# Two attention loops of a hybrid block: latent heads scored in pairs, and the first NSA head ahead of the compressed sums

## What is computed

```python
# NSA branch, 8 heads of 128; with 256 tokens every 64-block is selected
s = einsum('bqgrd,bngd->bgrqn', qb, kc) * scale            # 15 compressed keys
o_cmp = einsum('bgrqn,bngd->bqgrd', masked_softmax(s, ...), vc)
...                                                        # causal softmax over ks, vs: o_slc
...                                                        # causal softmax over kw, vw: o_win
o = gb[..., 0:1] * o_cmp + gb[..., 1:2] * o_slc + gb[..., 2:3] * o_win

# latent branch, 8 heads; 128 plain and 64 rotated dimensions of query and key
q_b = rms_norm(q_b, mla_q_norm)
k_b = rms_norm(k_b, mla_k_norm)
s = jnp.einsum('bqhd,bkhd->bhqk', qb, k) * scale           # over 192 dimensions
p = masked_softmax(s, kpos[None, :] <= t[:, None])
o = jnp.einsum('bhqk,bkhd->bqhd', p.astype(v.dtype), v)

x = x + gate_a * ((g_a * o_a + g_b * o_b) @ w_o)
```

## Times and profile before

| | us |
|---|---|
| median of 3 runs | 1046.87 |
| lowest, highest | 1045.39, 1047.06 |
| the profiled execution | 1046.69 |
| its span | 1044.9 |

### The profile page before, as it was taken

One profiled execution on the slowest core, in us unless ns is written; L12 is line 12 of the kernel. 1 busy time (PEld: TensorE's weight loads), 2 busy tenths in 40 slices (PEclk: granted clock), 3 DMA queues, 4 the chain that ended last, 5 costly groups with the idle time before them and its releaser, 6 DMA issues.

```text
span 1044.9 us, 23159 instructions
## 1 busy us (share of the span) xinstructions
PE 1017.8 (97%) x8513; PEld 960.6 (92%) x8513; DVE 556.5 (53%) x1167; ACT 619.9 (59%) x1118; POOL 688.9 (66%) x306
## 2 busy tenths in 40 slices
PE   7999999999999999999999999999989999999998
PEld 4899999988899989999999899998567699999998
DVE  2577724579875445555631642288576744444400
ACT  4565764477784466666654556754575556666642
POOL 2498898822249875988798388880041076988795
PEclk9999999999999999999999999999999999999999
DMA  9988788756357882777778379966211044656563
GB/s 379 380 300 279 272 305 296 258 183 210 133 176 233 284 295 88 273 241 236 238 238 273 109 272 351 365 233 209 84 60 41 1 153 128 209 195 196 163 214 113
DMA packets 62616, 226.43 MB, mean 217 GB/s; under 512 B 6960, under 2 KB 8272, under 8 KB 61264
## 3 DMA queue, kind: packets, MB, share of 16 engines
q1 hardware_dynamic: 61344, 221.23, 61.3%
q10 hardware_dynamic: 1200, 4.23, 1.3%
HBM read 224.35 MB, written 1.08 MB: 216 GB/s over the span
## 4 chain that ended last, share of the span: by engine, by line
PE 79%; issue 6%; POOL 5%; DVE 4%; ACT 4%; DMA 1%; ACTq 0%; DVEq 0%; POOLq 0%
PE psL L560 73%; POOL WL L512 5%; PE psO L560 3%; PE psS L560 2%; ACT WH L1178 1%; DMA ring<-wts 1%; PE psL L1115 1%; DVE SQ L2379 1%; ACT R L1296 0%; DVE X L2089 0%; DVE sm L2297 0%; PE psS L1061 0%; DVE psL L2088 0%; ACT psL L1719 0%; DVE sm L2296 0%
## 5 line engine op out<-in xcount | busy, mean ns | idle before, releaser
L512 POOL TENSOR_TENSOR WL<-ring,WH 128x1024 fp32r<-128x1024 f32 (+1 forms) x282 | 669.5, 2393 | 226.6 <-ACT WH L1178 176.9
L560 PE MATMUL psL<-HR,WH 128*128 128x256 f32 (+1 forms) x3096 | 514.1, 278 | 1.9 <-DVE HR L1834 1.1
L560 PEld LDWEIGHTS psL<-HR,WH 128*128 128x128 f32 (+1 forms) x3096 | 452.9, 187 | 7.7 <-issue 4.8
L560 PE MATMUL psL<-HR,WL 128*128 128x256 f32 x1536 | 396.5, 277 | 0.0
L1178 ACT ACTIVATE WH<-ring 128x1024 fp32r<-128x1024 f32 (+1 forms) x210 | 216.5, 1042 | 106.3 <-PE psL L560 71.3
L560 PEld LDWEIGHTS psL<-HR,WL 128*128 128x128 f32 x1536 | 275.3, 188 | 0.0
L560 PE MATMUL psL<-RR,WH 128*128 128x256 f32 x1356 | 205.3, 277 | 2.8 <-DVE RR L2019 1.2
L560 PEld LDWEIGHTS psL<-RR,WH 128*128 128x128 f32 x1356 | 185.3, 187 | 4.5 <-issue 2.8
L560 PE MATMUL psL<-RR,WL 128*128 128x256 f32 x672 | 144.9, 277 | 0.3 <-POOL WL L512 0.3
L2117 DVE SCALAR_TENSOR_TENSOR CT<-psL,par,CT 128x254 f32<-128x254 f32 (+1 forms) x176 | 80.8, 480 | 107.9 <-ACT CT L1490 102.8
L1481 ACT ACTIVATE WH<-ring 128x1024 fp32r<-128x1024 f32 (+1 forms) x88 | 92.9, 1058 | 71.6 <-PE psL L560 62.9
(11 more groups left out here) (278 smaller groups left out, 1091.7 us busy)
## 6 DMA issues: line engine op xcount, KB each, us to landing
ring<-wts SPq DMA_DIRECT2D x285, 512.0 KB, 4.2
adaring<-ada_w SPq DMA_DIRECT2D x80, 512.0 KB, 4.5
R<-ada_w SPq DMA_DIRECT2D x8, 1024.0 KB, 16.3
ring<-wts SPq DMA_DIRECT2D x16, 384.0 KB, 3.9
R<-cum_dram ACTq DMA_DIRECT2D x8, 512.0 KB, 4.2
R<-wts SPq DMA_DIRECT2D x8, 512.0 KB, 6.6
ring<-wts SPq DMA_DIRECT2D x8, 288.0 KB, 3.2
adaring<-wts SPq DMA_DIRECT2D x4, 512.0 KB, 6.8
```

Of the source, the lines that this page charges most:

```text
L512: nc.gpsimd.tensor_tensor(WL[:, k, 0:n], ring[:, k, 0:n], WH[:, k, 0:n].bitcast(F32), SUB).then_inc(lo_done, 1)
L560: return nc.tensor.matmul(out, lhsT, rhs, start=start, stop=stop)
```

## The change

Four edits.

- Layout: `QB` and `KB` hold all plain dimensions of the eight heads first, then all rotated ones (before, 192 columns a head). So two heads' rotated parts lie side by side, 128 columns, and are transposed at once: head 2k lands on partitions 0 to 63 and head 2k+1 on 64 to 127, queries and keys of both in one unit, copied by VectorE into `MR`. The turns have 12 units in place of 16. ScalarE copies the query units in two pieces, VectorE applies the query gain in two.
- Latent scores in pairs (`mla_pair`): plain products of both heads, then the rotated products of both, one on the lower and one on the upper 64 rows, then both masks. A pair takes two banks. Pairs 0 and 1 are issued in steps 0 and 1, four heads in four banks; pairs 2 and 3 behind the transposes of steps 3 and 5 and ahead of the values of these steps.
- The maximum of NSA head 0 stands on VectorE ahead of the compressed sums, its exponential on ScalarE behind that of the compressed scores; the compressed probabilities are finished behind the scaling of head 0 and the maximum of head 1 (`compressed_probabilities`, called from `nsa_outs(1)`). The transposes of the compressed probabilities move from step 2 to step 3 of TensorE's loop and from a scratch bank to `psO`, and ScalarE's copy of them from behind the exponential of head 1 to behind that of head 3.
- `second_layer_values` moves from behind key-value unit 1 to behind unit 3.

```diff
-PLAN.bare("mla_turns", 16)
+PLAN.bare("mla_turns", 12)
...
-                if n == 1:
-                    second_layer_values()
                 if n == 2:
                     turn_compressed_keys()
+                if n == 3:
+                    second_layer_values()
...
                 for i in range(min(first, 2), count + 3):
                     if first <= i < count:
-                        masked_scores(p0 + i, i, score)
-                    if i == 2 and lead_in:
+                        scores(i)
+                    if i == 3 and lead_in:
                         turn_cmp()
...
+                    if behind:
+                        behind(i)
                     if i >= 3:
...
-            for i in range(16):
-                pair, kind = divmod(i, 4)
+            for i in range(12):
+                pair, kind = divmod(i, 3)
...
+                    if kind == 1:
+                        src = (QB, KB)[hh][:, t, NH * HD + pair * P:NH * HD + (pair + 1) * P]
...
+            def mla_scores(i):
+                if i < 2:
+                    mla_pair(i)
+            def mla_behind(i):
+                if i in (3, 5):
+                    mla_pair((i + 1) // 2)
+            def mla_pair(pair):
+                i = 2 * pair
+                pe.wait_ge(turned, 8 + 2 * pair + 2)
+                pe.wait_ge(rope_turned, pair + 1)
+                outs = []
+                for e in range(2):
+                    u = head_unit(16 + i + e)
+                    bank_wait(u)
+                    outs.append(psL[:, u % 4, :])
+                for q0, lo, hi in ((0, 0, P), (P, P, 384)):
+                    for e in range(2):
+                        mm(outs[e][:, lo:hi], MQN[:, i + e, q0:q0 + P], MKN[:, i + e, 0:hi - lo], True, False)
+                    for e in range(2):
+                        r = ROPE * e
+                        mm(outs[e][:, lo:hi], MR[r:r + ROPE, pair, q0:q0 + P], MR[r:r + ROPE, pair, T:T + hi - lo], False, False)
+                    for e in range(2):
+                        last = mm(outs[e][:, hi - P:hi], identb[:, :], maskb[:, :], False, True)
+                        if q0 == P:
+                            last.then_inc(lin_done, 1)
...
-                if n == 6:
+                if n == 7:
                     act.wait_ge(cs_ready, 1)
                     cs3 = CS.rearrange("p (m n) -> p m n", n=32)[:, :, 0:NCMP]
                     A(cs3, cs3, ACT.Exp).then_inc(ce_ready, 1)
+                    head_exp(0, [1.0, 1.0])
...
-                    if n == 1:
+                    if n == 3:
                         turned_cmp()
...
             dve.sem_inc(cs_ready, 1)
+            head_max(0)
+            key_gain(6)
             dve.wait_ge(ce_ready, 1)
...
+                if i == 1:
+                    head_max(1)
+                    compressed_probabilities()
```

More of the change, by code:

```diff
@@ L1046, in _, with attend @@
                 masked_scores(n, n, nsa_score)
-            def attend(name, pname, obase, count, score, value, lead_in, p0, first=0, follow=None):
+            def attend(name, pname, obase, count, scores, value, lead_in, p0, first=0, follow=None, behind=None):
                 for i in range(min(first, 2), count + 3):
                     if first <= i < count:
-                        masked_scores(p0 + i, i, score)
-                    if i == 2 and lead_in:
+                        scores(i)
+                    if i == 3 and lead_in:
                         turn_cmp()
@@ L1083, in turn_cmp @@
                     for t in range(2):
-                        last = nc.tensor.transpose(out[:, g * T + t * P:g * T + (t + 1) * P],
+                        last = nc.tensor.transpose(psO[:, 1, g * T + t * P:g * T + (t + 1) * P],
                                                    CS[:, t * T + g * P:t * T + (g + 1) * P], pv("ident"))
-                last.then_inc(s_done, 1)
+                last.then_inc(ct_done, 1)
             def nsa_value(n):
@@ L1113, in _ @@
                     hh, t = divmod(n, 2)
-                    o = (2 * pair + hh) * QK + lo
-                    last = nc.tensor.transpose(out[0:wd, n * P:(n + 1) * P], src[:, t, o:o + wd], pv("ident"))
-                last.then_inc(lin_done, 1)
[L1118 to L1123, removed]
+                    if kind == 1:
+                        src = (QB, KB)[hh][:, t, NH * HD + pair * P:NH * HD + (pair + 1) * P]
+                    else:
+                        src = (QB, QB, KB)[kind][:, t, (2 * pair + hh) * HD:(2 * pair + hh + 1) * HD]
+                    last = nc.tensor.transpose(out[:, n * P:(n + 1) * P], src, pv("ident"))
+                last.then_inc(lin_done, 1)
+            def mla_scores(i):
[23 more added lines that the diff above has]
+                            last.then_inc(lin_done, 1)
             def mla_value(n):
@@ L1638, in turned_copy, with head_exp @@
                 act.sem_inc(turned, 1)
+            def head_exp(n, scales):
+                u = head_unit(n)
+                act.wait_ge(max_ready, n + 1)
+                b = 26 + 4 * (n % 2)
+                for t, (lo, hi) in enumerate(((0, P), (P, 384))):
+                    st.mark(A(psL[:, u % 4, lo:hi], psL[:, u % 4, lo:hi], ACT.Exp, scale=scales[t],
+                              bias=sm[:, b + t:b + t + 1], accum_out=sm[:, b + 2 + t:b + 3 + t]))
+                act.wait_ge(act_step, st.n)
+                act.sem_inc(exp_ready, 1)
             u0 = PLAN.at["uq"][1]
```

100 lines of the change are left out of this document (45 added, 55 removed).

## The result

The changed kernel took 1054.07 us (median of 4, 1053.12 to 1056.8) beside 1046.22 us for the kernel before (median of 4, 1045.39 to 1047.06): a ratio of 1.0073, interval 1.0048 to 1.0098. That is 7.9 us slower. The forecast, 1049.5 us with a range up to 1051.7, had the direction, and under half of the size. Timed again (run e12) it was 1.0069 (1.0044 to 1.0093).

What follows compares the result with a forecast made beforehand. The prediction took VectorE, not the busy TensorE, to set the latent loop's pace. Its terms -0.45 + 2.5 - 1.1 + 1.8 = +2.75 us on 1046.69 gave 1049.44, stated as 1049.5 us, range 1046.8 to 1051.7.

Steps and rivals of the forecast that it cites:

- Part 1: Value half of the compressed attention, moved later: TensorE no longer waits for its scratch bank, -0.45 us.
- Part 2: NSA loop start: first value product waits for the compressed copy, now behind the exponential of head 3, +2.5 us.
- the same turn from there on in both kernels: NSA loop behind the delayed first value product: turns equally long in both kernels, so nothing of the +2.5 is won back.
- Part 3: Turns ahead of the latent scores: 12 units for 16, first scores 5.9 us behind the first transpose, -1.1 us.
- Part 4: Latent scores on TensorE: rope products on different row halves run together, a pair takes 2.90 us in place of 4.16.
- (a): Rival on latent pairs: row halves don't run together, Part 5 becomes +3.7, total 1051.3 us; chance 0.16.
- Part 5: Latent loop: VectorE waits for values behind paired scores; product of head 2 at 19.3 against 17.5 us, +1.8.
- The tail is the same: Latent loop after the product of head 2: VectorE full in both kernels, 3.17 us a head, no further difference.
- (b): Rival on the NSA loop: the later compressed copy costs nothing, the 2.5 us go, total 1046.9 us; chance 0.15.
- (c): Rival on the latent loop: TensorE, not VectorE, sets it, 5.0 us of scores saved, total 1042.6 us; chance 0.08.
- the signs that the forecast wrote down: Expected in the profile, among others: 2 us or more idle ahead of the 32-row product, VectorE waits in the latent loop.

Runs made afterwards that it cites:

- e12: The changed kernel timed again, no edit; 1053.86 us, 1.0069 against the kernel before.
- e2: Changed kernel with ScalarE's copy of the turned compressed sums ahead of the exponential of NSA head 3 instead of behind it; 1050.71 us, 1.0058 against the kernel before.
- e1: Changed kernel with matmuls of ones filling TensorE's waits at the NSA start and in the latent loop; 1047.36 us, 1.0026 against the kernel before.
- e7: e6 plus 7 matmuls of ones ahead of the transposes of NSA head 0; 1043.82 us, 0.9976 against the kernel before.
- e10: Changed kernel with matmuls of ones filling TensorE's waits at the NSA start alone; 1051.52 us, 1.0053 against the kernel before.
- e6: Kernel before with later second-layer values and the 12-turn layout, but single latent scores and the old NSA start; 1045.01 us, 0.9985 against the kernel before.
- e4: Kernel before with the latent part alone (12 turns, paired scores), NSA start as before; 1050.75 us, 1.0049 against the kernel before.

## Why the forecast was wrong, step by step

- **Part 1, -0.45:** right. From the first product of the key units to the compressed scores (748.30 before) it took 13.05 us before and 12.53 after, and no wait stands ahead of the 128*32 products.
- **Part 2, +2.5:** the queues were right. The first 32-row product comes 29.80 - 27.59 = 2.2 us later, where parts 1 and 2 together said 2.05. It waited 2.40 us; the profile names no releaser for that ("issue"), but the copy behind the fourth exponential ended at 765.74, 0.09 ahead of the product at 765.83, and with the copy earlier (e2) the wait was gone:

```profile
764.10 0.34 ACT L1678 ACTIVATE psL<-psL,sm 128x128 f32<-128x128 f32 x1 [0.96 <-DVEq L2338]
...
765.14 0.60 ACT L1749 ACTIVATE R<-psO 128x512 f32<-128x512 f32 x1
```

  What the step left out is the 2.4 to 2.8 us behind it. It took "the same turn from there on in both kernels", and for the first two turns they were not the same, since TensorE was at 1.2 GHz. e1 shows 3.16 us there with the clock up.
- **Part 3, -1.1:** right; 5.88 us from the first transpose to the first score where 5.9 was worked out. The profile puts the 0.45 us ahead of that score down to VectorE (L2476), not to ScalarE as forecast; ScalarE's seventh copy, which the bank asks for, ended at 809.48 and VectorE's last at 809.46, so the two can't be told apart.
- **Part 4, 2.90 us a pair:** right. 812.55 - 809.62 = 2.93 us; at 3.54, with the two 64-row products one behind the other, rival (a) would have shown. The rule of the Trainium skill (TensorEngine Tiling (Array Packing), Key Properties) that tiles work in parallel holds here for two row halves in fp32.
- **Part 5, +1.8:** right as long as the clock stays up. Product of head 0 at 822.09 - 809.62 = 12.5 us (12.3 worked out) with 2.26 us of waiting. In e1 the product of head 2 comes at 822.22 - 802.74 = 19.5 us (19.3 worked out), and the loop takes 35.70 - 33.48 = 2.2 us longer. The VectorE row of e1:

```profile
822.22 0.42 DVE L2461 TENSOR_TENSOR CT<-R,psO 128x256 f32<-128x256 f32 x1 [1.47 <-PE psO L561]
```

  In the changed kernel head 2 came at 21.0, behind the slow pair 3, with 3.00 us of waiting:

```profile
822.09 0.42 DVE L2449 TENSOR_TENSOR CT<-R,psO 128x256 f32<-128x256 f32 x1 [2.26 <-PE psO L561]
...
830.64 0.42 DVE L2449 TENSOR_TENSOR CT<-R,psO 128x256 f32<-128x256 f32 x1 [3.00 <-PE psO L561]
```

  "The tail is the same" failed: after the wait at 837.30 the transposes, values and first output products ran at the lower level, and the loop ended 6.3 us later than before instead of 1.8.
- **Rivals.** (a) falls by the 2.93 us. (b) falls: from the first key product to the first latent transpose e1 is 65.32 - 63.21 = 2.1 us longer than before, so the later product was not caught up. (c) falls: with TensorE's work in the loop cut, VectorE's input set the end, as part 5 said. None of the three had the clock in it.

So the step that failed is the sum itself: it priced every wait at the time that it lasts, and gave nothing to the matmuls behind it, in part 2 with "the same turn from there on in both kernels" and in part 5 with "the tail is the same". -0.45, +2.5, -1.1 and +1.8 were measured as -0.5, +2.7, -1.1 and +2.2, together 3.2 to 3.3. A fifth term was missing: 2.8 us at the NSA start and 4.0 us in the latent loop, less 0.4 us that the NSA loop gives back (31.96 against 32.36). That makes 6.1 to 6.5 by the table, twice the rest. Only one of the waits behind it stood among the signs that the forecast wrote down, that ahead of the 32-row product.

What stays open: what decides whether the clock falls at a given wait in a given execution. It fell behind 1.54 us in e12's profile and stayed up there behind 1.95 us; in the first profile of the changed kernel it was the other way round (1.53 and 1.95). In e7's profile two waits of 0.92 and 0.97 us were enough, and 1.38 us late in the latent loop of before were not. The runs changed only whether TensorE had work.

## What to carry to other kernels

A change that lets TensorE stand still for 2 us can cost more than these 2 us: look at each new wait on TensorE, and add, as a second price, the work that follows it at half speed until the clock is back (2.4 to 2.8 us at the NSA start here). Before trusting a gain from less work on TensorE, ask whether the engine that then sets the pace leaves it idle: here pairs that cost TensorE 2.93 us in place of 4.16 made the latent loop 1.9 to 2.2 us longer, with the clock up. A few matmuls of ones in a wait are worth trying, since nobody reads them. Take neighbouring waits together: up to the scores of head 5, removing one of two gave 1.9 to 2.2 us (e2), filling both 2.5 to 2.8 (e10).

## What the runs showed of the hardware

- The clock fell behind waits of 0.35 and 2.20 us (e2), of 1.65 and 0.24 us (e6), of 1.81 and 0.64 us with 1.3 us of work between (e4), and of 0.92 and 0.97 us (e7). The half of a pair then took up to 1.85 times as long (3.18 against 1.72 us). The Trainium skill (TensorE: Matmul & The Clock Gate, HAM oscillation — how this bites in real kernels) describes such falls in a kernel that waits for DMA. In this case's traces the waits ahead of the falls were for other engines, none of them over 2.6 us, and the cost was as real.
- The same program meets the fall in some executions and not in others (27 of 87 for the kernel before), and these were 2.9 to 3.8 us slower. The mean granted clock of each execution tells them apart at 0.997 or 0.998 against 1.000; the page of one profiled execution can't say how often it happens, and that of e7, at 0.998, shows a 9 in all its 40 slices.
- Two 64-row products on different row halves ran together, a pair of latent heads in 2.93 us against 4.16 for two single ones.
